# A stick-breaking attention and convolution block: the four head pairs written out, the next pair's convolution input and k groups moved, beta products of two pairs on GpSimd

## The reference

```python
hn = _rmsnorm(h, mix_norm_g[i])
q, k, v, ca, cg = jnp.split(hn @ w_in, ...)
attn = _stick_breaking_attention(q, k, v)      # 8 heads of 64
conv = _conformer_conv(ca, cg, ...)            # 512 channels, 31 taps
h = h + concat([attn, conv]) @ w_out[i]
hn = _rmsnorm(h, ffn_norm_g[i])
h = h + (silu(hn @ w_gate) * (hn @ w_up)) @ w_down
return _rmsnorm(h, final_norm_g)[:, N_META:]
```

## Time and profile before

| what | value |
|---|---|
| median of 3 runs | 1293.82 us (1292.64 to 1296.67) |
| the profiled execution | 1292.03 us, its span 1290.3 |
| TensorE busy | 1210.6 us, 94% of the span |
| VectorE busy | 740.3 us, 57% |
| GpSimd busy | 494.2 us, 38% |
| ScalarE busy | 457.4 us, 35% |
| mean granted TensorE clock | 0.98 |
| chain that ended last | TensorE 58%, VectorE 16%, GpSimd 11% |

### The profile page before, as it was taken

The page is one execution under the profiler, slowest core; times in us unless marked ns, Lnnn a source line. Parts: engine busy times, 40 slices in busy tenths (PEclk is TensorE's granted clock), DMA queues, the critical chain, the costliest instruction groups (busy, mean ns, idle before and its releaser), DMA issues.

```text
span 1290.3 us, 16229 instructions
## 1 busy us (share of the span) xinstructions
PE 1210.6 (94%) x6108; PEld 1014.4 (79%) x6108; DVE 740.3 (57%) x781; ACT 457.4 (35%) x881; POOL 494.2 (38%) x374
## 2 busy tenths in 40 slices
PE   5999999999998869998999999999999999999996
PEld 4799879879877657886788778787878787878775
DVE  4337997997995993557644343433433434343446
ACT  4312462462561743454431322223131323141323
POOL 5212201101100151224582737465564747382921
PEclk9999999999998879998899999999999999999999
DMA  5404102102002401011212120212111212112113
GB/s 189 125 25 109 33 18 66 33 15 66 16 0 50 180 17 33 33 36 40 89 34 66 33 66 33 66 33 66 37 65 64 66 33 66 54 45 66 34 33 146
DMA packets 55554, 73.44 MB, mean 57 GB/s; under 512 B 1732, under 2 KB 45828, under 8 KB 55238
## 3 DMA queue, kind: packets, MB, share of 16 engines
q1 hardware_dynamic: 54310, 70.49, 17.5%
q10 hardware_dynamic: 1184, 2.13, 0.4%
HBM read 62.03 MB, written 6.32 MB: 53 GB/s over the span
## 4 chain that ended last, share of the span: by engine, by line
PE 58%; DVE 16%; POOL 11%; issue 9%; ACT 3%; DMA 2%; DVEq 0%; POOLq 0%; SPq 0%; ACTq 0%
PE ps L1586 18%; PE ps L1563 16%; PE ps L1394 13%; DVE gq L1111 7%; PE ps L1512 5%; POOL wa_lo L584 4%; PE ps L1352 4%; DVE acc L1068 3%; POOL wb_lo L584 2%; DVE wbeta L1116 2%; POOL wa_f L621 1%; PE ps L1452 1%; POOL wa_f L615 1%; POOL wa_f L618 1%; POOL wb_f L618 1%
## 5 line engine op out<-in xcount | busy, mean ns | idle before, releaser
L1275 DVE TENSOR_TENSOR mix<-ps,mix 128x512 f32<-128x512 f32 x176 | 121.3, 691 | 137.6 <-PE ps L1586 137.6
L1068 DVE SCALAR_TENSOR_TENSOR acc<-u_pad,parp,acc 128x1024 f32<-128x1024 f32 x116 | 157.3, 1400 | 0.2
L521 POOL TENSOR_TENSOR wp_lo<-raw,wp_hi 128x1024 fp32r<-128x1024 f32 x16 | 46.7, 2919 | 240.7 <-ACT wp_hi L684 176.1
L1586 PE MATMUL ps<-wd_hi,act_hi 128*128 128x512 f32 x352 | 137.0, 389 | 1.5 <-DVE act_lo L1264 1.5
L1586 PE MATMUL ps<-wd_hi,act_lo 128*128 128x512 f32 x352 | 136.9, 389 | 0.0
L1586 PE MATMUL ps<-wd_lo,act_hi 128*128 128x512 f32 x352 | 136.9, 389 | 0.0
L584 POOL TENSOR_TENSOR wa_lo<-wa_f,wa_hi 128x512 fp32r<-128x512 f32 x59 | 79.9, 1358 | 136.2 <-ACT wa_hi L893 132.4
L1394 PE MATMUL ps<-hn_hi,wp_hi 128*128 128x348 f32 (+2 forms) x352 | 119.3, 339 | 2.3 <-DVE par L1083 2.3
L1394 PE MATMUL ps<-hn_lo,wp_hi 128*128 128x348 f32 (+2 forms) x352 | 118.4, 336 | 0.0
L1394 PE MATMUL ps<-hn_hi,wp_lo 128*128 128x348 f32 (+2 forms) x352 | 118.2, 336 | 0.0
L1111 DVE TENSOR_TENSOR_SCAN gq<-gq,ones 128x1040 f32<-128x1040 f32 (+4 forms) x64 | 103.0, 1609 | 9.8 <-ACT wbeta L803 9.5
(11 more groups left out here) (162 smaller groups left out, 2761.6 us busy)
## 6 DMA issues: line engine op xcount, KB each, us to landing
raw<-in_w_gate SPq DMA_DIRECT2D x11, 1024.0 KB, 5.4
raw<-in_w_up SPq DMA_DIRECT2D x11, 1024.0 KB, 5.3
wd_f<-in_w_down SPq DMA_DIRECT2D x11, 1024.0 KB, 4.8
raw<-in_w_in SPq DMA_DIRECT2D x20, 512.0 KB, 3.9
kd<-kd SPq DMA_DIRECT2D x4, 1040.0 KB, 6.8
xin<-in_x SPq DMA_DIRECT2D x8, 512.0 KB, 3.6
wo_raw<-in_w_out SPq DMA_DIRECT2D x4, 1024.0 KB, 8.0
mix<-in_x SPq DMA_DIRECT2D x8, 512.0 KB, 4.0
```

Source lines behind the costliest of these rows:

```text
L521: pool.tensor_tensor(dst, raw[:, slot, :], hi.bitcast(F32), ALU.subtract).then_inc(wlo_done, 1)
L1068: dve.scalar_tensor_tensor(out=acc[:, j % 2, :], in0=u_pad[:, j:j + L], scalar=parp[:, j:j + 1], in1=acc[:, j % 2, :], op0=ALU.mult, op1=A ...
L1275: dve.tensor_tensor(hrow, ps[:, TB + n % 4, :], hrow, ALU.add).then_inc(d_added, 1)
L1586: last = pe.matmul(ps[:, TB + n % 4, :], a[s][:, t, i * P:(i + 1) * P], w_[m][:, t, dh * BANK:(dh + 1) * BANK], start=(t == 0 and s == m = ...
```

## The change

1. The four pairs are written out on every engine; waits count with `PROJ`, the list of all projections in order, instead of formulas.
2. The convolution input of the next pair is still made behind k and q, but `glu` and the taps stand elsewhere: 18 taps before the first pair; in a pair 19 (in the first 11) in the group stage, one behind each of the first five units (in the first pair three), and behind units 8 to 15 one tap of the next quarter (two in the third pair). In the last pair one behind each of the first twelve.
3. The k groups 0 and 1 of the next pair are issued at the last units: group 0 ahead of the attention of the last unit but one, group 1 ahead of that of the last; their splits follow at the pair's end. In the last pair the second q group is no longer held back.
4. In the third and last pair (`POOL_FROM = 2`) the beta products run on GpSimd. In exchange VectorE makes the low parts of `w_out`. The last weight's low part (q of the last pair) comes behind the third pair's products.
5. Output projection and FFN entry: layernorm's way back before the second half of the projection; `mix_lo` and the silu earlier; the last tile's projection ahead of the first two products; residual ahead of the T sums' low parts; T sums of tiles 6 and 7 interleaved; another order of the first weights.

```diff
+    PROJ = [(kind, g, 0) for kind, g in GROUPS[5:]] + [t for p in range(PAIRS) for t in groups_of(p)]
...
@@ block.gpsimd
-            def pair(p, more):
-                if more:
-                    for n in range(2):
-                        lo(CH_LOOP + 4 * p + n, n, wp(wp_lo, n), wp(wp_hi, n))
-                    pool.wait_ge(t_ready, past(NT * p + CT[2]))
...
+            def weigh(p, n):
+                w = width(UNITS[n][1])
+                pool.wait_ge(scanned, NU * p + n + 1)
+                pool.tensor_tensor(wbeta[:, n % BUFS, FRONT:FRONT + w - 1], wbeta[:, n % BUFS, FRONT:FRONT + w - 1],
+                                   gq[:, n % BUFS, 1:w], ALU.mult).then_inc(w_ready, 1)
+            for kind, p in WEIGHTS[4:-1]:
+                lo_weight(kind, p)
+            for p in range(POOL_FROM, PAIRS):
+                for n in range(NU):
+                    weigh(p, n)
+                if p == POOL_FROM:
+                    lo_weight(*WEIGHTS[-1])
...
+            pool.wait_ge(wo_ready, 2 * TILES)
             weight_sum(0, 5)
             weight_sum(0, 6)
+            h_root(TILES - 1)
+            weight_sum(0, 3)
             weight_lo(0, 5)
-            pool.wait_ge(wo_ready, 2 * TILES)
-            weight_sum(0, 3)
-            h_root(TILES - 1)
...
@@ block.vector, pair
+                for (kind, g), n in zip(GROUPS[2:5], (2, 2, 0)):
+                    split_lo(kind, g, p)
+                    some_taps(p, now, n)
+                if more:
+                    some_taps(p, now, len(now) - 8)
+                    glu(0, p + 1)
+                    some_taps(p, now, 2)
+                    glu(1, p + 1)
+                    some_taps(p, now, 1)
...
+                    if p < POOL_FROM:
+                        dve.wait_ge(scanned, NU * p + n + 1)
+                        dve.tensor_tensor(...)
+                    if more and n == 0:
+                        glu(2, p + 1)
+                    if more and n < 5:
+                        some_taps(p, now, 1)
                     elif more and n > 7:
-                        some_taps(p + 1, early, 1)
+                        some_taps(p + 1, ahead, 1 if p < POOL_FROM else 2)
                     elif not more:
-                        some_taps(p, rest, 1)
+                        some_taps(p, now, 1)
+                    if not more and n >= WO_AT + 2:
+                        w_out_lo(n - WO_AT - 2)
...
@@ block.vector, behind the tiles
+            residual(TILES - 1)
             t_low(1, "T1", 4, 6)
+            norm_h(TILES - 1)
+            lo_h(TILES - 2)
+            t_sum("T1", 6)
+            t_sum("T3", 6)
             t_low(2, "T2", 4, 6)
-            residual(TILES - 1)
...
@@ block.tensor
+            for p in range(PAIRS - 1):
+                pair(p, {NU - 1: lambda: groups(groups_of(p + 1)[:1]), NU: lambda: groups(groups_of(p + 1)[1:2])})
...
+                    ln_backward(i + 1)
                 w_out_part(i, 1)
                 if i >= 1:
                     transpose_h(i - 1)
-                if i + 1 < TILES:
-                    ln_backward(i + 1)
-
+            pe.wait_ge(hlo_ready, TILES // 2)
+            pe.wait_ge(h_ready, 2 * (TILES - 1) - 1)
+            product(0, 1)
+            pe.wait_ge(ln_norm, TILES)
+            product(0, 2)
+            transpose_h(TILES - 1)
             pe.wait_ge(h_ready, 2 * TILES - 1)
             product(1, 1)
```

More of the change, by code:

```diff
@@ L843, in pair @@
                         act.activation(wo_hi[:, k, :], wo_raw[:, k, :], ACT.Copy).then_inc(wo_hi_s, 1)
-                if not more:
+                if more:
+                    for g in range(2):
+                        split_hi("k", g, p + 1)
+                else:
                     mix_hi(1, 0)
                 evac_attention(1, NU - 1)
-            with act.Fori(0, PAIRS - 1) as p:
-                pair(p, True)
-            pair(PAIRS - 1, False)
+            for p in range(PAIRS):
+                pair(p, p + 1 < PAIRS)
             def ln_silu_of(i):
@@ L1084, in _, with w_out_lo @@
             for g in range(3):
-                glu(g, -1)
-            for j in range(EARLY):
-                tap(0, j)
+                glu(g, 0)
+            taps = [list(range(CONV_K + 1)) for _ in range(PAIRS)]
+            some_taps(0, taps[0], 18)
+            def w_out_lo(k):
+                dve.wait_ge(wo_hi_s, k + 1)
+                dve.tensor_tensor(wo_lo[:, k, :], wo_raw[:, k, :], wo_hi[:, k, :].bitcast(F32),
+                                  ALU.subtract).then_inc(wo_lo_s, 1)
             def mix_lo(i, part):
@@ L1203, in _ @@
                     residual(i - 1)
+                mix_lo(i, 1)
                 if i >= 2:
@@ L1473, in pair @@
                         transpose_w(n, range(2, nb))
-            def next_k(p):
-                pe.wait_ge(z_free, past(NZ * p + max(m + 1 for m in range(NZ) if Z_BANKS[m] == PJ)))
-                groups(p + 1, GROUPS[:1], True)
-            groups(0, GROUPS[:1], True)
-            with pe.Fori(0, PAIRS - 1) as p:
-                pair(p, True, lambda: next_k(p))
+            groups(groups_of(0)[:2])
+            for p in range(PAIRS - 1):
+                pair(p, {NU - 1: lambda: groups(groups_of(p + 1)[:1]), NU: lambda: groups(groups_of(p + 1)[1:2])})
             def ln_forward(i):
@@ L1533, in first_tile, with product @@
                 ln_backward(0)
-            def product(b, k, between=None):
+            def product(b, k):
                 n = NTH[b, k]
```

298 lines of the change are left out of this document (143 added, 155 removed).

## The result

The changed kernel takes 1310.25 us (median of 4, 1309.74 to 1313.04), the kernel before 1295.24 in the same measurement: ratio 1.0119, 95% interval 1.0103 to 1.0135. It is slower, as forecast, and inside the range, but by about twice the forecast 7.8 us. The profiled execution took 1309.9 us, its span is 1308.2, which is 17.9 more than before. That is the number to take apart, with one reservation. The medians differ by 15.0 us only: the profiled execution of the kernel before lies 3.2 us under the median measured here, so some 3 of the 17.9 us are differences between executions.

The account below looks back on a forecast made before the run. VectorE's queue from a pair's first scan to its last product was taken as the bound. Eight terms, 1.6 + 2.5 + 16.6 + 1 - 6.6 - 0.8 - 0.5 - 6, gave +7.8 us: 1301.6 us median, range 1287 to 1314.

Parts of the forecast that it names:

- Step 2: Second pair: five more taps in the units, +2.5 us; their leaving the group stage gains nothing.
- Step 8: FFN entry: earlier projection of the last tile and reordered products shorten TensorE's waits, -6 us (bounds 0 and -13).
- Steps 3 and 5: Unit stages of the third pair, +16.6 us, and of the last pair, -6.6 us.
- the product term: Third and last pair: beta products on GpSimd cost VectorE 2.06 ns a column, 19.5 us a pair.
- Step 1: First pair: 18 taps instead of 9 before the first k split, +1.5 us; unit stage +0.1; together +1.6.
- step 6: K groups between the last units: the first fills the last attention's wait, 0.25 us a pair, -0.8 in all.
- Step 4: Third to last pair: second q group stands in TensorE's wait for `kd`; +1 us.
- side by side rival: GpSimd products do not block VectorE; below 1.64 ns a column the whole is no slower; near 1264 us, chance 0.09.
- cold TensorE: Rival: full blocking (+7.6), half-level clock into the k groups, FFN entry gains only 2 us; near 1313, chance 0.17.

Follow-up runs that it names:

- e3: Changed kernel with the same taps elsewhere in VectorE's queue: more around the k splits, 6 instead of 12 in the run before the first convolution product; 1306.34 us.
- e4: Changed kernel with everything from the output projection on as it was before the change; 1310.38 us.
- e9: e4 with GpSimd's weight sums and low parts of the FFN's first two blocks replaced by fills that read nothing; 1300.14 us.
- e8: Changed kernel with GpSimd's weight sums and low parts of the FFN's first two blocks replaced by fills that read nothing; 1296.58 us.
- e1: Changed kernel with all beta products back on VectorE; 1299.87 us.
- e2: Changed kernel with only the third pair's beta products back on VectorE, the last pair's still on GpSimd; 1305.57 us.
- e6: e1 with the eight low parts of w_out on GpSimd, as before the change; 1309.14 us.
- e7: e1 with the convolution's taps moved out of the units into places where VectorE idled; 1265.12 us.
- e10: e7 with the third and the last pair's beta products on GpSimd; 1275.5 us.

## Why the prediction was right and wrong

The sign was right, and for its main reason: products on GpSimd block VectorE, which the unit stages go by. The size was off by 10.1 us in the profiled executions (17.9 instead of 7.8) and by 7.2 in the medians (15.0), by these steps.

- **Step 2, "the five taps come from the group stage, where TensorE is busy all the time; their leaving gains nothing".** That is the step that failed. It counted how many taps the group stage keeps and not where they stand. The order of the changed kernel's queue could be read beforehand: none between the k splits, two ahead of each q split, then twelve in one piece ahead of the first convolution product. It cost 4.3 us at each of two boundaries, where 0 was forecast (shown by e3; the whole kernel gained only 3.9 us there, since a part came back in the units). A TensorE that is busy in 48 of 48 us does not prove that an engine beside it is not about to become late.
- **Step 8, "-6".** Nothing came of it (e4). Its mechanism, a norm and a low part behind stretched T sums, was named, but the stretch was put at 2 us and one stall of 1; it was 7.3. The step's own terms also add up to 10.6 us (4.7 of chain, 2.9 of T sums, 3 of stalls) and not to "9 to 10". And it took the waits of the old order for a matter of order, where e9 shows them to be mostly GpSimd's stretch as well: with fills the new order is 1.5 us ahead, not 6. Of the two bounds, 0 and -13, the upper one came true; the 12.3 us of e8 are what the fills are worth, not the order.
- **Steps 3 and 5, the product term.** 19.5 us a pair were taken, 16.7 and 17.5 measured (e1, e2), in the main because a GpSimd product is shorter than the subtraction that it was priced by (1.77 ns a column against 2.09). The rest of the third pair came to +8.3 (55.9 less 47.55) where 10.1 was forecast; the rest of the last pair to -15.4 (56.7 less 72.1) where -13.1 was, 8.8 of it from `w_out`'s low parts (e6).
- **Step 1** was forecast at +1.6 and came to +3.5; the first scan's time differs by 2.7 us between executions with the same code up to there (146.7 us in e9, 149.4 in e4), so only the unit stage's +1.6 is sure. The step had that stage at +0.1 and the time ahead of it at +1.5; whether the 1.5 is there these runs don't show. **Step 2's** units (+2.5, measured +2.0) held, and **step 6** (0.25 a pair) fits the 0.3 of e3. **Step 4** was +1 and is +1 or +2.4 with the clock.

The errors partly cancel: 8.6 and 6.8 us too little for the boundaries and the entry, 4.6 and 4.3 too much for the two pairs. That the total stayed inside the range is luck to that extent. Of the text's own conditions, the third pair (59.6 us) stayed above 55 and its scans and taps were stretched, as it said; that the FFN's entry saves under 3 us was named as what would make it wrong, and did. The side by side rival (loss below 1.64 ns a column, the whole no slower) is refuted: the loss per pair is 1.76 and 1.85 ns a column, and the kernel slower; that of the cold TensorE gave the nearest total, but by another way: the clock in the third pair was 0.91, and in the last it rose from 0.83 to 0.97.

## What to carry to other kernels

When work is moved between queues, write down for the engine that is full not only how much it has in a stage but in what order, and where it will idle: putting the taps where VectorE idled was worth 34.8 us (e1 to e7), the products' way back 10.4 (e1, e10). Work that an engine does beside another one is only free where they can both read; a price for it should come from rows of the same operation, or be given as a range where there are none. And a gain on a chain that a third engine stretches is not there until that engine's work is out of its way.

## What was unexpected in the hardware

- A GpSimd fill, which reads nothing, stretches no VectorE instruction (e8: 0.68 and 1.29 us beside fills of 0.53), where a subtraction of the same 512 columns adds 1.1 us.
- A VectorE instruction that takes one operand from PSUM is not stretched by a GpSimd sum beside it. Changed kernel, the residual (two rows, 1.28 us in e8 beside no GpSimd read) and GpSimd:

```profile
611.63 1.67 DVE L1222 TENSOR_TENSOR hn2f<-hn2f 128x512 f32<-128x512 f32 x1
613.22 1.27 DVE L1186 TENSOR_TENSOR mix<-ps,mix 128x512 f32<-128x512 f32 x2
```
```profile
612.83 1.63 POOL L627 TENSOR_TENSOR wb_f<-wb_f,raw 128x512 f32<-128x512 f32 x1
```

- The T sum ahead of it, with both operands in SBUF, took 1.67 instead of 0.69. But a plain tap (one tensor and a column of factors, all in SBUF) was stretched as well in the third pair, from 0.74 us (e1) to 2.28.
